# Seven block products instead of eight in the second block's input projection

## The reference

```
h = rmsnorm(x, norm_pre_g)
z = h @ w_in                       # 1024 -> 4096
q, k, v, g_attn, c_h, c_b, c_c, g_conv = split(z)   # 4 x 768, then 4 x 256
q, k = rope(q), rope(k)            # rotation by the position, heads of 64
attn_out = dilated_attention(q, k, v) * silu(g_attn)
conv_out = c_b * causal_conv3(c_c * c_h) * silu(g_conv)
x = x + rmsnorm(concat(attn_out, conv_out) @ w_out, norm_post_g)
```

## Time and profile before

| what | value |
|---|---|
| median of 3 runs | 2241.88 us (2238.7 to 2242.82) |
| span of the profiled execution, first to last instruction | 2236.8 us |
| median of the runs less that span | 5.1 us |
| TensorE busy | 2059.5 us, 92% |
| DVE busy | 1394.6 us, 62% |
| ACT busy | 925.3 us, 41% |
| POOL busy | 912.2 us, 41% |
| granted TensorE clock, mean | 0.977 |

### The profile page before, as it was taken

The page is one execution under the profiler, slowest core; times in us unless marked ns, Lnnn a source line. Parts: engine busy times, 40 slices in busy tenths (PEclk is TensorE's granted clock), DMA queues, the critical chain, the costliest instruction groups (busy, mean ns, idle before and its releaser), DMA issues.

```text
span 2236.8 us, 43330 instructions
## 1 busy us (share of the span) xinstructions
PE 2059.5 (92%) x16228; PEld 1509.7 (67%) x16228; DVE 1394.6 (62%) x3479; ACT 925.3 (41%) x2009; POOL 912.2 (41%) x1004
## 2 busy tenths in 40 slices
PE   5999999996988999699999999999989888786998
PEld 3545868885887887588544444746877777665886
DVE  7714949765997465773466772222199999894422
ACT  4323334221886011332233331212189999882211
POOL 4312323373423998431112212211133888984222
PEclk9999999998999999899999999999999999998999
DMA  5442321356642233332344341321157887674552
GB/s 183 141 113 63 104 82 39 90 146 197 152 113 105 89 134 126 123 124 72 128 139 121 111 116 62 121 56 63 53 126 167 207 202 194 172 205 148 161 177 85
DMA packets 285536, 279.95 MB, mean 125 GB/s; under 512 B 39712, under 2 KB 237216, under 8 KB 285072
## 3 DMA queue, kind: packets, MB, share of 16 engines
q1 hardware_dynamic: 281280, 271.08, 42.2%
q0 software_dynamic: 1680, 5.51, 0.7%
q10 hardware_dynamic: 2368, 0.60, 0.1%
HBM read 171.22 MB, written 93.31 MB: 118 GB/s over the span
## 4 chain that ended last, share of the span: by engine, by line
PE 31%; DVE 21%; POOL 11%; issue 5%; DMA 3%; ACT 3%; SPq 2%; DVEq 0%; ACTq 0%; POOLq 0%
PE bank L173 20%; PE bank L2641 7%; DVE s2m L2491 6%; DVE p2l L2497 4%; POOL xr L1776 2%; POOL xr L1763 2%; POOL xr L1761 2%; POOL xr L1778 2%; SPq L1964 1%; DMA qr<-qf 1%; PE bank L1405 1%; DVE qf L1933 1%; DVE qr L1931 1%; DVE qf L1930 1%; ACT s2sh L1915 1%
## 5 line engine op out<-in xcount | busy, mean ns | idle before, releaser
L173 PE MATMUL bank<-xh,w2h 128*128 128x512 f16 x640 | 243.3, 380 | 0.0
L173 PE MATMUL bank<-xl,w2h 128*128 128x512 f16 x640 | 243.2, 380 | 0.0
L173 PE MATMUL bank<-xh,w2l 128*128 128x512 f16 x640 | 243.1, 380 | 0.0
L173 PE MATMUL bank<-w2h,xh 128*128 128x256 f16 x768 | 210.4, 274 | 14.6 <-DVE xl L638 13.6
L173 PE MATMUL bank<-w1h,xh 128*128 128x256 f16 x768 | 211.0, 275 | 3.0 <-DVE s1st L937 3.0
L173 PE MATMUL bank<-w1h,xl 128*128 128x256 f16 x768 | 210.8, 275 | 0.0
L173 PE MATMUL bank<-w1l,xh 128*128 128x256 f16 x768 | 210.8, 274 | 0.0
L173 PE MATMUL bank<-w2l,xh 128*128 128x256 f16 x768 | 210.4, 274 | 0.0
L173 PE MATMUL bank<-w2h,xl 128*128 128x256 f16 x768 | 210.3, 274 | 0.0
L2436 PE MATMUL bank<-ident,p2r 128*128 128x128 f32 x900 | 163.7, 294 | 49.0 <-DVE p2l L2497 41.8
L260 POOL TENSOR_TENSOR size<-size,power 128x1 f32<-128x1 f32 x15 | 8.6, 570 | 398.3 <-DVE size L254 398.3
(11 more groups left out here) (375 smaller groups left out, 5632.6 us busy)
## 6 DMA issues: line engine op xcount, KB each, us to landing
scr_part<-ob SPq DMA_DIRECT2D x48, 264.0 KB, 3.4
cm<-scr_part SPq DMA_DIRECT2D x48, 264.0 KB, 4.8
v<-scr_v SPq DMA_DIRECT2D x192, 65.0 KB, 2.7
w2r<-in_w_in SPq DMA_DIRECT2D x12, 1024.0 KB, 6.8
qr<-qf SPq DMA_DIRECT2D x192, 64.0 KB, 2.0
ax<-in_x SPq DMA_DIRECT2D x16, 512.0 KB, 6.3
xr<-in_x SPq DMA_DIRECT2D x16, 512.0 KB, 4.5
bx<-scr_x SPq DMA_DIRECT2D x16, 512.0 KB, 7.9
```

The lines of the kernel that those rows point to most:

```text
L173: ins = nc.tensor.matmul(dst, x, y, start=k == 0 and m == 0, stop=k == n - 1 and m == 2)
```

## The change

Input and weights of a chunk are cut in two along the inner dimension, along the positions and along the columns, and the chunk's product is made by the scheme of Strassen and Winograd: seven products of halves instead of eight. The 13 chunks behind the values use it.

1. *Sums of the activations.* For each half P of the sequence (1024 positions; a and b are its first and second 512) the norm stage makes T1 = B12 - B11, T2 = B22 - T1, T3 = T2 - B11 and T4 = B21 - T2 from `xh` and `xl` (9 operations of DVE on 4 x 512 elements), a high part of each (ACT) and a remainder (POOL). T1 takes the place of B12 in `xh` and `xl`, once the value groups that read it are through. The hand-written order is changed: the third value chunk goes (2,1), (2,3), (2,0), (2,2), and the sums and the first split stand among the groups.
2. *Sums of the weights.* POOL no longer casts and subtracts 2048 elements. It makes S1 to S4 (four operations of 512), ACT casts the high parts of A (1024), A22, S1, S2, S3, S4 (512 each), and POOL subtracts the remainders, in eight steps spread over the slots 4 to 11 of the chunk before. ACT still scales the raw weights first.
3. *Products and their sums.* A chunk has 2 x 7 products of 12 matmuls ("f", 512 columns) or 48 (gates, 128 columns). Each group of seven uses three banks of six. Products four to seven add into the bank of an earlier one, and each waits until that bank's earlier content has been read: by ACT (`m1`) or by an addition of DVE from PSUM (`u2`, `u4`, a result). The other two banks serve the weights' totals and bounds.
4. *Rotation stage.* ACT evicts one result of four, DVE's additions make the others. Turn, high part and remainder of a tile come 2, 3 and 4 slots (products) behind its result; there are five `qf` and three `qr`. The three operations of the rotation are DVE's, as before.
5. *Stages.* The gate stage is cut in a mix stage (four chunks) and a gate stage (three), with a stage's end between them. The first weight buffer shares its memory with `q0`, so the loads of `q0` wait for chunk 14's weights. The stage's scratch tile for the sum of squares is gone; ACT writes that output to `hi`.

```diff
+    SEVEN = ((0, 0, "B11"), (4, 1, "T2"), (5, 2, "T3"), (3, 1, "T1"), (1, 0, "B21"), (6, 1, "B22"), (2, 2, "T4"))
+    CORNERS = (("C22", 1, 1), ("C11", 0, 0), ("C12", 0, 1), ("C21", 1, 0))
+    def pe_product(kind, wts, n, i, xs, bank):
+        (wh, wl), (op, _, name) = wts.parts(n), SEVEN[i]
+        xh, xl = xs[name]
+        for u in range(1 if kind == "f" else 4):
+            dst, cols = (bank[:], slice(0, 512)) if kind == "f" else (bank[:, 128 * u:128 * u + 128], slice(128 * u, 128 * u + 128))
+            for k in range(4):
+                for m, (w, x) in enumerate(((wh, xh), (wh, xl), (wl, xh))):
+                    a, b = w[:, op, k, :], x[:, k, cols]
+                    ins = nc.tensor.matmul(dst, *((a, b) if kind == "f" else (b, a)), start=i < 3 and u == k == m == 0,
+                                           stop=k == 3 and m == 2, skip_group_check=True)
...
+        def act_prep(self, n, step):
+            def cast(name):
+                src, hi, _ = p[name]
+                nc.scalar.activation(hi, src, ACT.Copy).then_inc(*self.a_w.up())
+            # step 0: A, A22; 1: S3, S1; 4: S2; 7: S4
+        def pool_prep(self, n, step):
+            # step 0: add(0, a11, a21, subtract); add(1, a21, a22, add)    1: rest("A22")    2: rest("S3")
+            # 3: add(0, S1, a11, subtract)    4: rest("S1")    5: rest("A")
+            # 6: add(1, a12, S2, subtract); rest("S2")    7: rest("S4")
...
-        work += [("split", 2), ("group", 1, 3)]
-        work += [("consts",), ("load", 3)]
-        work += [("group", 2, 0), ("total", 3), ("group", 2, 1), ("scaled", 3), ("group", 2, 2), ("group", 2, 3)]
+            work += [("split", 2), ("pair", 0, "T4"), ("group", 1, 3), ("pair", 0, "T3"), ("load", 3), ("pair", 1, "T1"), ("group", 2, 1),
+                     ("kept", 0), ("total", 3), ("pair", 1, "T2"), ("scaled", 3), ("bound", 3), ("group", 2, 3), ("prep", 3, 0), ("pair", 1, "T4"),
+                     ("prep", 3, 1), ("prep", 3, 2), ("group", 2, 0), ("fit", 3), ("prep", 3, 3), ("prep", 3, 4), ("pair", 1, "T3"),
+                     ("kept", 1), ("prep", 3, 5), ("prep", 3, 6), ("prep", 3, 7), ("group", 2, 2)]
...
+    def slots_of(n_chunks, outs, after, weights):
+        for at in range(14 * n_chunks + 8):
+            i, s = divmod(at, 7)
+            if i < 2 * n_chunks:
+                work.append(("mul", i, s))
+                if s in (1, 2):
+                    work.append((("t", i), ("u2", i))[s - 1])
+                if s == 4:
+                    work.append(("u4", i))
+            done = (i - 1, 3) if s == 0 else (i, s - 4) if s >= 4 else None
+            if done is not None and 0 <= done[0] < 2 * n_chunks:
+                work += [(x, *done) for x in outs]
+                for later, what in after:
+                    due.setdefault(at + later, []).append((what, *done))
+            work += due.pop(at, [])
+            if i < 2 * n_chunks:
+                work += [(what, at // 14, *more) for slot, what, *more in weights if slot == at % 14]
+    PREPARE = [(0, "load"), (0, "sum"), (1, "total"), (3, "scaled"), *((4 + k, "prep", k) for k in range(8))]
...
     def rope_stage(scope, wts, first, xs, xs_ready, fits):
+        work = slots_of(6, ("out",), ((2, "turn"), (3, "half"), (4, "rest")),
+                        PREPARE + [(5, "bound"), (7, "pbound"), (9, "fit")])
...
+                    if s == 0:
+                        pe.wait_ge(*wts.ready[first + n])
+                    pe.wait_ge(*xs_ready[P].get(SEVEN[s][2], before))
+                    pe.wait_ge(*(before if s < 3 else (d_u.at(5 * i + 1), a_t.at(i + 1), d_u.at(5 * i + 2), d_u.at(5 * i + 3))[s - 3]))
+                    pe_product("f", wts, first + n, s, xs[P], bank).then_inc(*p_mm.up())
...
+        def dve_add(dst, i, bank, mm, to):
+            dve.wait_ge(*p_mm.at(7 * i + mm))
+            nc.vector.scalar_tensor_tensor(dst[:], trio[i][bank][0][:], fits.fit[:, i // 2:i // 2 + 1], to[:], ALU.mult, ALU.add).then_inc(*d_u.up())
```

More of the change, by code:

```diff
@@ L356, in norm_stage @@
             work.append(("turn", g))
+            if late and g == 3:
+                work.append(("pair", 0, "T1"))
             if g == 0:
@@ L366, in norm_stage @@
                     work.append(("turn_v", g - 1))
+            if late and g == 3:
+                work.append(("pair", 0, "T2"))
             work.append(("group", 0, g))
@@ L1847, in rope_stage, with made @@
+        trio = trios(12, lambda i: (a_q.at(i + 1), d_u.at(5 * i + 4), d_u.at(5 * i + 5)))
+        small, total_bank = Banks([6, 7]), {}
+        for item in work:
+            if item[0] == "total":
+                total_bank[item[1]] = small.take(wts.total[first + item[1] + 1])
+            elif item[0] == "pbound" and item[1] < 5:
+                fits.take(item[1] + 1, small)
         N = len(tiles)
+        def made(m):
+            i, q = divmod(m, 4)
+            return (d_u.at(5 * i + 3), a_q.at(i + 1), d_u.at(5 * i + 4), d_u.at(5 * i + 5))[q]
@@ new lines, in mix_stage, with of, mul_at @@
+        m1, u2, u4 = (sbs(n, 2, [128, 512], F32, scope) for n in ("m1", "u2", "u4"))
+        work = slots_of(4, ("out",), ((1, "times"), (2, "tail"), (3, "last")), PREPARE)
+        for n in range(4):
+            wts.spent[first + n] = p_mm.at(14 * n + 14)
+        def of(i):
+            return i // 2 % 2 == 0, i // 4, i % 2, 2 * (i // 4) + i % 2
+        def mul_at(i, q):
+            conv, c, P, _ = of(i)
+            return g_mul.at(6 * c + (2 * P + q - 1 if conv else 4 + P + 1))
+        trio = trios(8, lambda i: (d_u.at(6 * i + 4), d_u.at(6 * i + 5), d_u.at(6 * i + 6)))
@@ new lines, in sp_program @@
+        def sp_program():
+            for item in work:
+                if item[0] == "load":
+                    wts.sp_load(first + item[1] + 2)
+                elif item[0] in ("tail", "last") and item[2] >= 2 and not of(item[1])[0]:
+                    what, i, q = item
+                    _, c, P, j = of(i)
+                    b = q - 2
+                    s = 1024 * P + 512 * (1 - b)
+                    if what == "tail":
+                        sp.wait_ge(*a_bh.at(2 * j + 1 + b))
+                        nc.sync.dma_start(c2h[128 * c:128 * c + 128, s:s + 512], f(hbuf[b][:])).then_inc(*h_out[b].up(16))
+                    else:
+                        sp.wait_ge(*d_bl.at(2 * j + 1 + b))
+                        nc.sync.dma_start(c2l[128 * c:128 * c + 128, s:s + 512], f(lbuf[b][:])).then_inc(*l_out[b].up(16))
```

858 lines of the change are left out of this document (586 added, 272 removed).

## The result

| | before | after |
|---|---|---|
| median of 4 runs | 2242.1 us (2238.7 to 2242.8) | 2285.3 us (2283.1 to 2288.8) |
| ratio | | 1.0198 (1.0179 to 1.0217) |
| span of the profiled execution | 2236.8 us | 2281.4 us |
| mean granted TensorE clock | 0.977 | 0.957 |

The forecast was 2247 us with a range to 2272. The direction was right, the size was missed by 38 us.

What follows compares the result with a forecast made beforehand. TensorE was taken to set the pace, DVE nearest behind. Terms -74 + 40 + 15 + 14 + 1 + 7 + 2 = +5 on 2241.8 gave 2247 us; forecast's own range 2238 to 2258, 8-in-10 range 2218 to 2272.

Steps and rivals of the forecast that it cites:

- products removed: Dense stretch from rotation to attention: 14 products per chunk instead of 16 half-tiles, 548.3 us falling to 474, -74 us.
- 5 rest: Mix and gates: +1 us each for waits of TensorE on DVE's additions and POOL's extra work, +2 us together.
- rival C: Gates: 128-column products run at 81 ns because weight loads don't hide, 51 us more, 2298 us; chance 0.03.
- step 2: Rotation stage: POOL's weight split hits DVE some 4.7 us a chunk, making DVE late and TensorE stall, +15 us.
- the slack of slots 10 to 13: Rotation chunks: late slots repay DVE's lateness of about 2 us with queries and 2.8 with keys.
- rival B: Rotation: DVE becomes the bound, 7.5 of POOL's 12.6 us a chunk hitting it, plus late landings; 2269 us, chance 0.15.
- I count nothing for it: Rotation: SP queue's shuffles and stores, 29 us in 36.2, taken as hidden; 0 us, 0 to 6 in the range.
- step 4: TensorE clock: half rate after long idle stretches loses 3.4, 2 and 1.6 us, none after 2 us stalls; +7 us.
- step 3: Two changes of stage: TensorE waits after two products for the next weights' total, +10 and +4 us, +14 together.
- step 1: Norm stage: sums of activations and first weight split delay the first rotation product from 1074.1 to 1114 us, +40 us.

Runs made afterwards that it cites:

- e15: Changed kernel with three buffers per stored half, POOL's weight sums and remainders for five chunks and DVE's sine product cut to 8 columns: 2234.6 us.
- e11: Changed kernel with POOL's ten weight sums and remainders per rotation chunk moved to DVE, and three buffers per stored half: 2264.7 us.
- e17: e11 plus normalisation's end on DVE, sum-of-squares product one slot later, DVE's rotation order evened out, first rotation chunk's sum of squares earlier: 2250.5 us.
- e1: Changed kernel with three buffers for each stored half in the rotation stage instead of two: 2273.8 us.
- e2: Changed kernel with POOL's ten weight operations per chunk cut to 8 columns for five chunks, leaving most of that work out: 2257.7 us.

## Why the prediction was wrong by 38 us

| step of the prediction | forecast | measured | how |
|---|---|---|---|
| products removed | -74 | -74 | pitches 0.2156 and 0.056 |
| 1 norm stage | +40 | +37.2 | 1111.3 - 1074.1 |
| 2 stalls of the rotation | +15 | +38.5 | 56.0 - 17.5 |
| 3 changes of stage | +14, +1 | +17.9 | waits of 11.7 and 6.2 |
| 4 clock | +7 | about +22.3 | 17.5 in the rotation, 13 products x 0.216 = 2.8 in the mix, some 2 in the gates |
| 5 rest | +2 | +2.5 | what is left of 118.4 = 592.3 less the 473.9 of products |

**Right**: the removed products, with the pitch that the last four products of the trace promised, so that rival C did not come: the 81 ns of the Trainium skill, "TensorE: Matmul & The Clock Gate", "Back-to-back issue gap", don't hold for these products at 56 ns. Right too were the first rotation product (1114 forecast, 1111.3 seen) with the wait before it, the kind of each stall, and its place behind the second products.

**Wrong, step 2**: +15 was to come from 4.7 us of POOL's time a chunk that hits DVE, repaid by "the slack of slots 10 to 13". The three groups of turns exceed 0.69 us by 324, 308 and 136 ns, eight tiles a chunk: 6.1 us, between the forecast's 4.7 and rival B's 7.5. DVE's whole load came as forecast: 210.8 us busy in the stage and some 12 behind it on the last four tiles are 37.1 us a chunk, and the prediction's terms make 31.5 or 34.2 plus 4.7, 37.5 on average. What failed is the step from the load to the stalls. The lateness was not repaid: in the stage DVE was idle for 62 us, 16.9 of them in front of its remainders, for the stores of earlier ones, and 37.5 for products of TensorE, which had itself stood still behind late additions. "I count nothing for it" on the SP queue was the second error of the step: the third buffer was worth 11.5 us, and 15 once POOL was away, with the same burst of shuffles that the prediction had worked out (14 us in 10.4). The row that showed it was at hand: landings were compared with when DVE wants a shuffle, not with when ACT wants back a stored half, of which there are two.

**Wrong, step 4**: "The stalls of 2 us inside the chunks get none" was right for three of the four stalls of 2 to 3 us, but five stalls grew to 5 to 6.6, and each of these was followed by the lower clock for 9 to 13 products. (The 3.4 us for one long gap were about right: 14 products at the stage's start cost 3.0. The "some 7 us at half rate" are more than the earlier trace rows hold, where TensorE is busy for 0.57 us in the first window and for 5.00 in the second.) The step took the size of the stalls from step 2 as certain. e15 shows that the 17.5 us were a consequence: it kept 9 slow products of 81. The two steps missed 23.5 + 15.3 = 38.8 us, the size of the whole error; +3 in step 3 and -3 in step 1 cancel.

**Rival B** was the nearest by its number: DVE as the bound, a hit of 7.5 us a chunk and late landings, 2269 us, and 2284 with the 15 of clock that it lacked. Part of that is luck. Chunks of 39 and 41.7 us against 36.2 give 3 x 2.8 + 3 x 5.5 = 25 us by its own terms, not the 33 that it counted, and DVE was not busy all the time, as a bound would be, but idle for 62 us of the stage. It deserved more than 0.15 even so, as 6.1 us of 7.5 came true and the queue's burst did cost time, though at the stores and not at the shuffles' landings, and the range, whose upper end was near B's value, had to hold what follows a stall.

What stays open: e11 to e17 still have 24 to 30 us of waits in the rotation. DVE's load there is some 37.8 us a chunk (in e11 214.9 us busy in the stage and 12 on the last four tiles) against 36.2 of products. An estimate from these two alone would be 10 us over six chunks, and in e17's stage DVE is idle for 30. So what makes the rest of these waits, load, order or the waits of DVE itself, is not shown; no kernel here has all the arithmetic and a lighter DVE.

## What to carry to other kernels

When fewer products are bought with elementwise work, add up that work per chunk against the shorter chunk, and price the engines that exclude each other as one: here 28 of the 43 us went away with POOL's work beside DVE, and 11 with a third of DVE's turns. Price a stall with what follows it: here a wait of TensorE of 5 to 6.6 us cost 2 to 3 more in clock. And for each buffer ask who needs it back, not only who needs what it holds: a queue that issues a burst of one kind holds up the stores of the other, and through them an engine which has nothing to do with either.

## What the runs showed of the hardware

- A product of 128 columns that loads its own weights holds a pitch of 0.056 us over whole gate chunks (0.45 us over eight).
- DVE operations with one operand from PSUM stay at 0.745 us whether POOL is busy 106 us of the stage or 43, those with two operands in SBUF go from 0.69 to 0.83 to 1.01 on average, and with the sine on POOL (busy 174 us of the stage) to 1.18 and 1.29.
- An operation of DVE on 128 x 8 elements, 0.17 us alone, took 1.15 us while POOL worked:

```profile
1259.44 1.15 DVE L2021 TENSOR_TENSOR qwm<-qwm,most 128x8 f32<-128x8 f32 x1
```

This row is from e1's timeline of DVE; the 0.17 us is the mean of five in e2.

- A subtraction of 512 columns took 1.41 us on average on POOL beside DVE's work (changed kernel) and 0.68 on DVE (e11).
